# A two-layer hybrid encoder step on one core: the beginning of both layers rearranged, averages of squares in fp32, norms by root and reciprocal

## The reference

```python
h = rms_norm(xp, ln_mix[l])      # x * rsqrt(mean(x*x) + 1e-6) * g
qa, ka, va, la, qb, kb, vb = project_heads(h, w_in[l], b_f[l])   # la = log_sigmoid(h @ w_f + b_f)
o = concatenate([fox_prompt(qa, ka, va, la), swa_prompt(rope(qb), rope(kb), vb, sinks)])
xp = xp + o @ w_out[l]
mk, mv = memory_kv(mem_prompt, ln_memtok[l], w_mk[l], w_mv[l])   # has an RMS norm of its own
xp = xp + cross_attend(rms_norm(xp, ln_mem[l]), w_mq[l], mk, mv, w_mo[l])
xp = xp + conv_ffn(rms_norm(xp, ln_ffn[l]), w_up[l], w_conv[l], b_conv[l], w_down[l], ...)
```

## Time and profile before

| | |
|---|---|
| time, median of 3 runs | 3394.49 us (3394.02 to 3395.08) |
| profiled execution: its time | 3398.06 us |
| profiled execution: its span | 3396.3 us |
| TensorE matmuls busy | 3238.6 us (95%) |
| VectorE, GpSimd, ScalarE busy | 1896.0 (56%), 1210.1 (36%), 844.5 us (25%) |
| share of the chain that ended last on TensorE | 80% |

### The profile page before, as it was taken

How to read it: one execution, slowest core, us unless ns; L and a number is a source line. 1 busy time by engine, 2 the same in 40 slices (tenths; PEclk the granted TensorE clock), 3 DMA queues, 4 the chain that set the end, 5 groups by cost and what they waited for, 6 DMA issues and landing times.

```text
span 3396.3 us, 50293 instructions
## 1 busy us (share of the span) xinstructions
PE 3238.6 (95%) x20496; PEld 3119.4 (92%) x20496; DVE 1896.0 (56%) x3536; ACT 844.5 (25%) x1960; POOL 1210.1 (36%) x976
## 2 busy tenths in 40 slices
PE   7999999999999999999999999989899999999997
PEld 7888898888899999999988988978889999999997
DVE  6555567676754444444665655576667444444446
ACT  4432333553310000000233333154433000000002
POOL 5213222632443333334342222334424333334331
PEclk9999999999999999999999999999999999999998
DMA  4111222210111111111122112221101111111111
GB/s 159 45 58 45 61 59 68 66 44 29 35 47 45 46 44 44 44 44 47 41 78 58 45 38 64 75 73 48 50 26 44 45 44 44 44 44 47 44 44 64
DMA packets 86021, 177.57 MB, mean 52 GB/s; under 512 B 10544, under 2 KB 13872, under 8 KB 85392
## 3 DMA queue, kind: packets, MB, share of 16 engines
q1 hardware_dynamic: 71968, 132.90, 13.4%
q10 hardware_dynamic: 13824, 41.46, 4.2%
HBM read 150.36 MB, written 16.29 MB: 49 GB/s over the span
## 4 chain that ended last, share of the span: by engine, by line
PE 80%; DVE 11%; ACT 5%; issue 2%; POOL 1%; DMA 0%; SPq 0%; ACTq 0%; DVEq 0%; POOLq 0%
PE PS L611 80%; DVE ACC L1628 2%; ACT PR L1256 1%; DVE HL L1620 1%; DVE PR L1709 1%; DVE XT L1752 1%; ACT PW L1256 1%; DVE PW L1709 1%; DVE XT L1582 1%; ACT PTH L1108 1%; POOL WL L591 1%; DVE PTL L1554 0%; POOL WH L589 0%; DVE DG L1667 0%; ACT G0H L1108 0%
## 5 line engine op out<-in xcount | busy, mean ns | idle before, releaser
L589 POOL TENSOR_TENSOR WH<-RAW,zero 128x512 fp32r<-128x512 f32 x484 | 548.6, 1134 | 2100.7 <-PE PS L611 2086.0
L611 PE MATMUL PS<-HH,WH 128*128 128x384 f32 (+1 forms) x3312 | 865.0, 333 | 43.5 <-DVE HL L1620 17.1
L611 PE MATMUL PS<-HL,WH 128*128 128x384 f32 (+1 forms) x3312 | 849.0, 328 | 0.0
L611 PE MATMUL PS<-HH,WL 128*128 128x384 f32 (+1 forms) x3312 | 849.0, 328 | 0.0
L591 POOL TENSOR_TENSOR WL<-RAW,WH 128x512 fp32r<-128x512 f32 x484 | 666.4, 1377 | 38.0
L611 PEld LDWEIGHTS PS<-HH,WH 128*128 128x128 f32 x3312 | 587.7, 189 | 61.6 <-issue 19.3
L611 PEld LDWEIGHTS PS<-HL,WH 128*128 128x128 f32 x3312 | 590.8, 189 | 0.0
L611 PEld LDWEIGHTS PS<-HH,WL 128*128 128x128 f32 x3312 | 589.7, 188 | 0.0
L1752 DVE TENSOR_TENSOR XT<-PS,XT 128x320 f32<-128x320 f32 x464 | 314.1, 718 | 264.7 <-PE PS L611 264.5
L611 PE MATMUL PS<-G0H,WH 128*128 128x384 f32 (+1 forms) x960 | 275.4, 339 | 25.4 <-DVE XT L1582 16.6
L1108 ACT ACTIVATE PTH<-PS 128x512 fp32r<-128x512 f32 (+4 forms) x320 | 165.4, 520 | 530.8 <-PE PS L611 529.5
(11 more groups left out here) (255 smaller groups left out, 4715.9 us busy)
## 6 DMA issues: line engine op xcount, KB each, us to landing
RAW<-in_slabs SPq DMA_DIRECT2D x484, 256.0 KB, 2.6
XR<-decays ACTq DMA_DIRECT2D x16, 512.0 KB, 5.8
XT<-in_xT SPq DMA_DIRECT2D x8, 544.0 KB, 8.4
out_fk<-T ACTq DMA_DIRECT2D x8, 544.0 KB, 2.7
XR<-decays ACTq DMA_DIRECT2D x16, 272.0 KB, 7.0
out_fv<-T ACTq DMA_DIRECT2D x8, 544.0 KB, 2.8
out_y<-YT ACTq DMA_DIRECT2D x8, 544.0 KB, 3.2
RX<-ST ACTq DMA_DIRECT2D x24, 136.0 KB, 4.0
```

The source lines that it names most:

```text
L589: pool.tensor_tensor(WH[:, s, :], RAW[:, s, :], zero[:, 0:1].to_broadcast([128, HALF]), ALU.add).then_inc(w_hi, 1)
L611: ins = pe.matmul(*a, **k)
```

## The change

- **First projection by tiles** (layer 0): `project_first` does f tile by tile as each arrives, and the averages of squares in four pieces between, each over the sum of two tiles' squares.
- **fp32 averages**: `stat`, `mem_stat` and `first_stat` multiply the unsplit fp32 sums with the fp32 matrix. The splits before them go.
- **Norm**: `R` is the root (ScalarE, in two parts) and then VectorE's `reciprocal` of 768 and 320 columns. A dummy `Exp` (`exp_table`) follows in most places.
- **Queries ahead of keys**: the order is f, q0, k0. The sample's own scores of pair 0 (`own_scores`) move behind the first value part, since the keys come later.
- **First values as parts**: v0 is done in the gaps of pair 0 as in the other pairs; its `value_hook` moves from step 0 to step 2.
- The cumulative sum over the cache is made before the queries leave PSUM, the gate bias is added in other instructions, and the memory's norm moves ahead of k0.

```diff
-    order = ["f", ("k", 0), ("q", 0), ("v", 0)]
+    order = ["f", ("q", 0), ("k", 0)]
     for p in range(PAIRS):
-        order += [("ck", p), ("v", p), ("cv", p)] if p else [("ck", p), ("cv", p)]
+        order += [("ck", p), ("v", p), ("cv", p)]
...
+            def project_first(pe, key):
+                s = claim(pe)
+                for kt in range(KT):
+                    if kt % 4 == 0:
+                        slot = slab(pe, key)
+                    pe.wait_ge(h_ready, kt + 1)
+                    c = slice((kt % 4) * 128, (kt % 4 + 1) * 128)
+                    products(pe, s, [[(w[:, slot, c], x[:, kt, :]) for w, x in ((WH, HH), (WH, HL), (WL, HH))]], CH,
+                             kt == 0, kt == KT - 1)
+                    if kt == 3:
+                        signal(w_used, now=True)
+                    if kt in (2, 4, 6):
+                        first_stat(pe, kt // 2 - 1)
+                done(s)
+                signal(w_used)
+                first_stat(pe, KT // 2 - 1)
+            def first_stat(pe, pair):
...
+                pe.wait_ge(sq_used, pair + 1)
+                for (a, b), o in zip(CH, STAT):
+                    mm(pe, PS[:, o:o + b - a], mean, FIRST_SQ[2 * pair][:, a:b], start=pair == 0, stop=pair == KT // 2 - 1)
...
             def stat(pe):
-                pe.wait_ge(stat_ready, place.at("norm", 1))
+                pe.wait_ge(sq_used, place.at("norm", KT - 1, KT - 1))
...
-                for k, x in enumerate((SH, SL)):
-                    for (a, b), o in zip(CH, STAT):
-                        mm(pe, PS[:, o:o + b - a], mean_r[:], x[:, a:b], start=k == 0, stop=k == 1)
+                for (a, b), o in zip(CH, STAT):
+                    mm(pe, PS[:, o:o + b - a], mean, ACC[:, a:b], start=True, stop=True)
...
+                    if s < 0 and steps[0]["kind"] == "fox_s" and steps[0]["late"]:
+                        pe.wait_ge(attn_ready, place.at("attn", 1))
+                        place.add("attn")
+                        own_scores(pe)
...
-                project(pe, "f", HH, HL, CH, fresh=0)
+                if l == 0:
+                    project_first(pe, "f")
+                else:
+                    project(pe, "f", HH, HL, CH, fresh=0)
                 place.add("ntile", KT)
-                project_late(pe, ("k", 0))
-                project(pe, ("q", 0), HH, HL, CH)
-                own = project(pe, ("v", 0), HH, HL, CH)
+                project_late(pe, ("q", 0), stat if l else lambda pe: None)
+                if l == 0:
+                    mem_stat(pe)
+                project(pe, ("k", 0), HH, HL, CH)
...
-            def inverse_rms(act):
+            def rms(act):
                 act.wait_ge(stat_done, place.at("norm", 1))
                 act.activation(like(R, 0, 768), PS[...], 
-                               ACT.Ln, bias=eps[:])
-                wait_own(act, act.activation(R[:, 768:T], PS[:, STAT[2]:STAT[2] + T - 768], ACT.Ln, bias=eps[:]))
-                act.activation(R[:], R[:], ACT.Exp, scale=-0.5).then_inc(rms_ready, 1)
+                               ACT.Sqrt, bias=eps[:]).then_inc(rms_ready, 1)
+                act.activation(R[:, 768:T], PS[:, STAT[2]:STAT[2] + T - 768], ACT.Sqrt, bias=eps[:]).then_inc(rms_ready, 1)
...
+            def exp_table(act):
+                act.activation(SM[:, 0, 0:1], one[:], ACT.Exp)
...
                 filled(act)
-                hi(act, [(QH[:], QLS)])
+                hi(act, [(KH[:], STAGES[0])])
+                act.dma_start(o_fk[l * PAIRS], STAGES[0]).then_inc(k0_out, 16)
                 biases(0)
...
+            def invert_rms(dve):
+                dve.wait_ge(rms_ready, place.at("norm", 1, 2))
+                dve.reciprocal(R[:, 0:768], R[:, 0:768])
+                dve.wait_ge(rms_ready, place.at("norm", 2, 2))
+                wait_own(dve, dve.reciprocal(R[:, 768:T], R[:, 768:T]))
...
-                if kt > 1:
-                    add_squares(dve0, kt - 1, kt - 1)
-            add_squares(dve0, KT - 1, KT - 1)
-            split_sums(dve0)
-            masks(dve0)
+                if kt % 2:
+                    dve0.wait_ge(sq_ready, kt + 1)
+                    dve0.tensor_tensor(FIRST_SQ[kt - 1], FIRST_SQ[kt - 1], FIRST_SQ[kt], ALU.add)\
+                        .then_inc(sq_used, KT // 2 if kt == KT - 1 else 1)
+            memory_sums(dve0)
...
-                    before = {2: lambda: place.add("store")} if pair else {}
-                    hooks = {2: own_values} if pair else {0: own_values}
+                    before = {2: lambda: place.add("store")}
+                    hooks = {2: own_values}
```

More of the change, by code:

```diff
@@ L201, in encoder_step @@
         mean_r = sb("mean_r", [128, 128], F32R)
+        mean = mean_r[:].bitcast(F32)
         causal_r = sb("causal_r", [128, 128], F32R)
@@ L692, in project, with project_late @@
                 return filled
-            def project_late(pe, key):
+            def project_first(pe, key):
[15 more added lines that the diff above has]
+            def first_stat(pe, pair):
+                if pair == 0:
+                    pe.wait_ge(g_free, place.at("group", 2))
+                    pe.wait_ge(o_free, place.at("step", 1))
+                pe.wait_ge(sq_used, pair + 1)
+                for (a, b), o in zip(CH, STAT):
+                    mm(pe, PS[:, o:o + b - a], mean, FIRST_SQ[2 * pair][:, a:b], start=pair == 0, stop=pair == KT // 2 - 1)
+                if pair == KT // 2 - 1:
+                    signal(stat_done, now=True)
+                    place.add("norm")
+            def project_late(pe, key, between):
                 s = claim(pe)
@@ L835, in mem_stat @@
             def mem_stat(pe):
[L837 to L841, removed]
+                pe.wait_ge(msq_used, 1)
+                pe.wait_ge(rms_ready, 2)
+                for c in range(2):
+                    mm(pe, PS[:, (6 + c) * 512 + 384:(7 + c) * 512], mean, MACC[:, c * 128:(c + 1) * 128], start=True, stop=True)
+                signal(mstat_ready, now=True)
             def value_tiles(pe, src, tiles_of, rows_of, filled):
@@ L917, in scores, with own_scores @@
                     signal(w_used)
[L918 to L922, removed]
+                    if not st["late"]:
+                        own_scores(pe)
+            def own_scores(pe):
+                pe.wait_ge(g_free, place.at("group", 1))
+                b = (6 + place.n["group"] % 2) * 512
+                out = PS[:, b:b + DEC]
+                for k, (q, key) in enumerate(((QSH, KH), (QSH, KL), (QSL, KH))):
+                    mm(pe, out, q[:], key[:, SEQ:T], start=k == 0, stop=False)
+                mm(pe, out, ident_r[:], tail_mask_r[:], start=False, stop=True)
+                signal(g_full, now=True)
+                place.add("group")
             def transposes(pe, st, s):
@@ L1282, in down @@
                     place.add("third")
-                if gains is not None or last:
-                    split_sums(act)
             def rope_swap(act, base, k):
@@ L1676, in attention @@
                 for s in range(n + 3):
-                    if s and ahead:
+                    early = s > 0 if ahead else s == 0 and steps[0]["late"]
+                    if early:
                         parts_out(s - 1, 2)
@@ L1772, in down @@
                     add_squares(dve, KT - 1, KT - 1)
-                if gains is not None or last:
-                    split_sums(dve)
             def rope(dve, base, k, nth, out):
@@ L1848, in own_values @@
                     value_groups(dve, V_GROUPS, own_rows)
-                keys()
-                fill(dve, QLS, stored=False)
-                queries()
-                if l == 0:
-                    memory_sums(dve)
-                fill(dve, T32)
-                place.add("store")
+                fill(dve, STAGES[0], stored=False)
+                lo(dve, [(KL[:], STAGES[0], KH[:])]).then_inc(attn_ready, 1)
+                place.add("attn")
                 for pair in range(PAIRS):
                     n = len(fox_steps(pair))
-                    before = {2: lambda: place.add("store")} if pair else {}
-                    hooks = {2: own_values} if pair else {0: own_values}
-                    if l == 0 and pair == 0:
-                        hooks[2] = lambda: place.add("use")
+                    before = {2: lambda: place.add("store")}
+                    hooks = {2: own_values}
                     if pair < PAIRS - 1:
```

132 lines of the change are left out of this document (58 added, 74 removed).

## The result

The changed kernel takes 3427.3 us (median of 4 runs, 3426.3 to 3431.5) against 3394.8 for the kernel before on the same chip: ratio 1.009, interval 1.0069 to 1.0111. It is slower by 32 us, where 17 us of gain were forecast. The profiled executions tell the same: 3398.06 before, 3428.12 after, at a mean granted clock of 0.988 in both.

What follows compares the result with a forecast made beforehand. TensorE, busy for 95% of the span, was taken to bound the kernel, through its waits and half-clock time. Terms summed to -17.0 us: 3398.06 to 3381.1, less 3.57 for the median, 3377.5; likeliest range 3368 to 3387.

Steps and rivals of the forecast that it cites:

- the price of the reciprocals: In each norm, the two reciprocals of R (768 and 320 columns) take 1.5 us together, 3.0 at the high end.
- the part on the norms: Five norms: stops of 1.8 us go, averages cost 0.85 us more, waits of 0.2 go in three; -5.35 us.
- The term of -3.4: Behind two norms, at 919 and its like in layer 1, half-clock stretches go with the stop: 1.7 us each.
- The rival of slow reciprocals: Norms: reciprocals at an eighth of the addition's rate take 9.2 us and stop TensorE; about 3425 us, chance 13%.
- threshold of 5.5 us: Norms: the price of both reciprocals together, 5 ns a column, from which it decides the sign of the change.
- The averages: Norms: an fp32 average takes 1.95 us instead of 1.1, and the 1.8 us stop before it goes in five.
- R's path: Norms: R is ready 2.5 us after the average instead of 3.9; a 0.2 us stop goes in three.
- The start: Start of layer 0: matmuls from 10.3, scores of pair 0 at 57.5 instead of 58.97; a gain of 1.5 us.
- Pair 0: From its first scores to step 4: 35.6 us in both layers, as in pair 1; gains of 4.8 and 1.5.
- the stop for GpSimd's split (1.0): Pair 0: v0's second slab can't be split before k0's last matmul; TensorE stops 0.9 us, 1.0 with margin.
- the cover of the bias: Pair 0: the bias lands about 10.5 us after the first scores, needed only after 19; cover some 7 us.
- the third rival: Pair 0: the bias is late and value exits queue behind the first probabilities; 3 us each layer, 3383, chance 5%.

Runs made afterwards that it cites:

- experiment 9: The changed kernel with the reciprocal of the last 320 columns made in pieces of 4, 8, 16, 32, 64 and 196; no kernel time given.
- experiment 4: The kernel before with only the averages changed to fp32 over the unsplit sum, R as before: 3385.3 us, ratio 0.9979.
- experiment 1: The changed kernel with each reciprocal of R replaced by a multiplication of the same columns, so the output differs: 3387.7 us, ratio 0.9982.
- experiment 6: The kernel of experiment 4 with the first projection done tile by tile and its average in four pieces: 3383.3 us, ratio 0.9974.
- experiment 7: The kernel of experiment 2 with v0 projected whole before pair 0, queries still ahead of keys: 3382.2 us, ratio 0.9970.
- experiment 5: The kernel of experiment 2 with the last gate sums ahead of q0's split and the bias loads ahead of k0's exit: 3385.5 us, ratio 0.9969.
- experiment 10: The kernel of experiment 2 with the edits of experiment 5 and experiment 7 together: 3384.6 us, ratio 0.9981.
- Experiment 2: The changed kernel with R made as before, by two logarithms and an exponential on ScalarE: 3394.9 us, ratio 1.0005.

## Why the prediction was wrong, point by point

**The step that failed** is the price of the reciprocals in the part on the norms: "I take 1.5, nearer to the additions". It is 7.05 us, and the high end, 3.0, did not hold it either. Both ends came from rows that could not bear it. The addition is another operation. The step between 156 and 159 ns was read as a slope of 3 ns a column, but experiment 9 shows 6.25 in pieces of `R`, and 119 ns for four columns: the small reciprocals of the attention are no start of that line. The rest of the mechanism was right. With 7.05 us in it, the prediction's own sum has R 5.55 us later, stops of 5.55 - 1.2 = 4.35 us in five norms, which is what was measured, and 5.55 in the last: +27, so 3405. Of what is still missing, some 9 us are the half clock at these stops and the rest is mainly pair 0. The term of -3.4 for two half-clock stretches that should go had rested on there being no stop: in experiment 4 they are gone, in the change they are longer (4.5 us of work each instead of 3.3).

The rival of slow reciprocals had the mechanism and the place, and got 13%. Its time, 3425 for 3427, is partly luck: it had 9.2 us instead of 7.05, stops of 6.5 instead of 4.4 and 4 us at the start of layer 0, where TensorE waits 0.2 for FZ; what made up for that were the half-clock stretches, which it counted at some 4 us, and pair 0, which it did not have. The argument against it ("a second column should add some 8 ns, and adds 3") set two kinds of instruction side by side that experiment 9 tells apart. Its threshold of 5.5 us for both was passed. A repeat count of 8, as the Trainium skill has it (VectorE: DVE Perf Modes, "First, the fixed hardware budget"), gives by my estimate eight additions' time, 10 us; the runs show 5.5 of them. I had set it below the row; it pointed the right way, and it was the only source on instructions of many columns.

**The averages** were right. 1.99 us was predicted as 1.95, the QL stops are gone in five norms, the stop at the last norm is 4.04 and its average 3.76. Alone they give 6 to 7 us (experiment 4), where the terms without R's shortening (5 x (0.85 - 1.8) - 3.4 - 0.8 for the last norm) make 9.

**R's path.** With the cheap operation of experiment 1 the window from 750 to 763 us in layer 0, the memory norm, holds no idle time of TensorE and the full clock. So the step was right but for its one term. It is worth little: TensorE waited only 0.2 for R before.

**The start** was forecast as -1.5 and is -0.2. The first matmul is at 11.38, not 10.3. PE and VectorE there:

```profile
11.38 0.98 PE L610 MATMUL PS<-HH,WH 128*128 128x384 f32 x2 [11.38 <-DVE HL L1653]
...
17.67 0.76 PE L610 MATMUL PS<-HH,WH 128*128 128x384 f32 x3 [1.70 <-DVE HL L1653]
```

```profile
8.92 4.36 DVE L1653 SCALAR_TENSOR_TENSOR HL<-XT,LCS,HH 128x1088 fp32r<-128x1088 f32 x2 [4.88 <-ACT HH L1330]
13.20 2.37 DVE L1833 TENSOR_TENSOR ACC<-ACC,SQ 128x1088 f32<-128x1088 f32 x1
15.49 2.12 DVE L1653 SCALAR_TENSOR_TENSOR HL<-XT,LCS,HH 128x1088 fp32r<-128x1088 f32 x1
```

The first HL ends at about 11.2. VectorE's passes take 2.1 to 2.4 us here instead of 1.3, and so the first tile is late by 0.9 and a later one by 1.7. The duration was taken from a row of before, and who else ran beside it was not asked. GpSimd's split of weights did, in both kernels. Before:

```profile
9.11 2.29 POOL L591 TENSOR_TENSOR WL<-RAW,WH 128x512 fp32r<-128x512 f32 x1
```

and after:

```profile
8.81 1.26 POOL L590 TENSOR_TENSOR WL<-RAW,WH 128x512 fp32r<-128x512 f32 x1
```

Before, VectorE starts first (8.92) and takes its 1.35, and the split takes 2.29; after, the split starts first and takes its 1.26, and VectorE's pass, again at 8.92, takes 2.31. The one that starts second pays. Where both overlap at the start of experiments 1, 6 and 7 it is the same; no run was made to isolate it. The stop of 4.37 at 20.8 is gone, as forecast. TensorE got 7.8 us of averages where it had 1.1, and the two nearly cancel: -0.2 here, and no gain that can be told in experiment 6.

**Pair 0** was forecast by the pattern of pair 1 (35.6), and the stop for GpSimd's split (1.0) is 1.4 to 1.7. The step that failed is the cover of the bias: "land 5.8 us after the issue", "needed only 19 us after them" and "The cover is some 7 us". The four loads are issued one behind another on ScalarE, from 1749.26 to 1751.5, while the weights for the next slabs arrive. From the profile after, ScalarE's queue and VectorE's wait, and then what TensorE pays:

```profile
1749.26 0.36 ACTq L1362 DMA_DIRECT2D XR<-decays  x1
...
1763.26 1.28 DVE L1742 CUSTOM_DVE_ANT_0 PR<-PS,XR,big 128x1024 f32<-128x1024 f32 x1 [8.32 <-DMA XR<-decays]
...
1766.72 0.64 PE L610 MATMUL PS<-HH,WH 128*128 128x320 f32 x1 [5.39 <-DVE T L1610]
```

The bias is usable 14.0 us after its first issue, not 5.8, and 16.3 us after the first scores (1746.93), not 10.5. In layer 0 it is 9.9 and 13.5. The time of need was wrong too. TensorE may want the probabilities late, but VectorE works in order, and behind the first exponential stands the exit T of a value part, for whose bank TensorE stops at 1761.3, 14.4 us after the first scores. The exit ends and TensorE goes on 3.5 us after the bias is there, so the bias had to be there at about 10.9 us: the cover was 0.4 us and not 7. In the kernel before it was 11.0 us, with v0's matmuls beside them:

```profile
1741.66 0.36 ACTq L1329 DMA_DIRECT2D XR<-decays  x1
...
1752.67 1.28 DVE L1709 CUSTOM_DVE_ANT_0 PR<-PS,XR,big 128x1024 f32<-128x1024 f32 x1 [0.40 <-DMA XR<-decays]
```

So VectorE holds the values' exit T behind the late first probabilities, as the third rival said ("the value exits queue behind them"), and TensorE stops; behind that it has 12.3 us at half clock. The rival named the wait but not its cause (the sums and q0's exit; it was the transfer) and not the clock: it asked 3 us a layer, and in layer 1 it is 7.9 more than before. Experiments 5 and 7 remove the wait in two ways and both come to 0.997.

**What stays open.** Experiments 4 to 7 and 10 lie between 0.9969 and 0.9981 with intervals that overlap, so that which of them is best, and whether start and parts of values add anything to the averages, can't be told. The 3377.5 of the forecast was reached by no median. Experiment 2 is some 8 us behind experiment 1; R's path, longer by 1.35 us at the last norm and by stops of 0.2 to 0.4 at five others (1.5 in all), makes 2.9 of them. The spans of their profiled executions are only 1.3 us apart (3394.4 and 3395.7); the rest is open. Why the clock falls for 3.4 us at one stop of 4.4 and for 6.7 at another, no run settles.

## What to carry to other kernels

A price by column can't be read from instructions of one and two columns at another place of the program: here these took longer than one of four columns did where the price mattered, and an upper bound taken from them bounded nothing. A run with a few sizes at the place itself settles it. Where work is taken away ahead of a stage, ask which transfer it was hiding, and time that from the issue of the first load to its use, with the traffic of that moment; and ask what stands behind the waiting instruction in its engine's order, since that can be needed sooner than its own result. A suspected edit is best run from both sides, undone on the new kernel and alone on the old: here they told the same loss (36.6 and 38 us).

## What the runs showed of the hardware

- An fp32 reciprocal on VectorE takes some 94 ns and 6.25 to 6.4 ns a column of 128 partitions: 128x4 119 ns, 128x196 1320, 128x320 2095, 128x768 4953. An addition of 128x1088 takes 1.28 us. Reciprocals of one and two columns in the attention took 156 and 159 ns.
- Stops of 4.3 to 5.4 us of TensorE came with 3.4, 6.7 or 13.5 us at half the clock (1.2 GHz instead of 2.4), which began 0.4 us behind the stop in the first case and inside it in the others.
- Four loads of the bias (272 to 512 KB each) took 9.4 to 14.0 us from the first issue to use with weights on the way, where the median of one was 5.8 (512 KB) and 7.0 us (272 KB) in the kernel before.
- At the start, a VectorE pass of 128x1088 took 1.35 us when it began before GpSimd's split beside it, and 2.31 when it began after; the split 2.29 and 1.26.
